# Expert tokens fetched by indirect transfers instead of one-hot products, in a mixture-of-experts decoder step

## The reference, cut to what matters

```
hid = jax.nn.silu(jnp.einsum('td,edf->tef', t, w_gate[g])) * jnp.einsum('td,edf->tef', t, w_up[g])
out = out + jnp.einsum('tef,efd->td', hid * comb[:, g, :, None], w_down[g])
```

## Time and profile before

| | us |
|---|---|
| median of 3 runs (lowest, highest) | 894.69 (891.93, 895.97) |
| the profiled execution: its time | 897.72 |
| the profiled execution: its span | 895.9 |
| rounds of layer 0, first `gate_up` to last `down` | 252.3 to 499.5 |
| rounds of layer 1 | 623.4 to about 864 |
| TensorE busy | 788.6 (88%) |
| VectorE, ScalarE, GpSimd busy | 423.2, 280.2, 128.6 |
| weight queue (q1): MB, share of the 16 DMA engines | 271.74, 77.1% |

### The profile page before, as it was taken

How to read it: one execution, slowest core, us unless ns; L and a number is a source line. 1 busy time by engine, 2 the same in 40 slices (tenths; PEclk the granted TensorE clock), 3 DMA queues, 4 the chain that set the end, 5 groups by cost and what they waited for, 6 DMA issues and landing times.

```text
span 895.9 us, 22455 instructions
## 1 busy us (share of the span) xinstructions
PE 788.6 (88%) x9194; PEld 470.6 (53%) x9195; DVE 423.2 (47%) x1134; ACT 280.2 (31%) x562; POOL 128.6 (14%) x214
## 2 busy tenths in 40 slices
PE   3799998999889999987886779976999979989984
PEld 2478886585545545443433448743545434545443
DVE  1149989515525444443331571262545434534544
ACT  2145674403223323232131251141232323223223
POOL 0160778000001010100000000000100100100001
PEclk9799997899879999999897879996999999999987
DMA  9997545428994998999999999398499999999301
GB/s 317 390 248 278 188 166 170 140 94 302 412 417 154 373 367 351 423 421 423 421 422 414 377 374 343 127 373 335 181 365 428 416 427 417 426 417 428 151 1 48
DMA packets 63885, 280.47 MB, mean 313 GB/s; under 512 B 3013, under 2 KB 3627, under 8 KB 55638
## 3 DMA queue, kind: packets, MB, share of 16 engines
q1 hardware_dynamic: 60738, 271.74, 77.1%
q0 software_dynamic: 2432, 6.94, 2.5%
q10 hardware_dynamic: 676, 1.24, 0.5%
HBM read 277.47 MB, written 3.37 MB: 313 GB/s over the span
## 4 chain that ended last, share of the span: by engine, by line
PE 66%; DMA 21%; DVE 5%; ACT 3%; SPq 2%; issue 2%; POOL 0%; POOLq 0%; DVEq 0%; ACTq 0%
PE bank L662 17%; DMA ring<-in_w_up 15%; PE bank L783 8%; PE bank L672 7%; PE bank L920 6%; PE bank L684 6%; PE bank L634 6%; DMA big<-in_w_up 3%; PE bank L529 3%; DMA ring<-in_w_ada 2%; DVE t L1260 2%; PE bank L577 2%; PE bank L569 1%; PE bank L642 1%; SPq L438 1%
## 5 line engine op out<-in xcount | busy, mean ns | idle before, releaser
L1677 DVE SCALAR_TENSOR_TENSOR x<-bank,ada,x 128x256 f32<-128x256 f32 x392 | 162.0, 476 | 0.0
L662 PE MATMUL bank<-ring,big 128*32 128x256 f32 x2112 | 136.2, 401 | 28.8 <-DMA ring<-in_w_up 22.9
L1674 DVE TENSOR_TENSOR big<-big,bank 128x32 f32<-128x32 f32 x98 | 18.4, 188 | 247.0 <-PE bank L684 247.0
L662 PEld LDWEIGHTS bank<-ring,big 128*32 128x32 f32 x2112 | 66.2, 114 | 89.4 <-issue 35.6
L1831 POOL TENSOR_TENSOR big<-t 128x192 f32<-128x192 f32 x51 | 26.5, 519 | 594.2 <-PE bank L634 430.4
L634 PE MATMUL bank<-htm,big 128*32 128x256 f32 (+1 forms) x1224 | 83.5, 386 | 4.8 <-POOL big L1834 4.8
L684 PE MATMUL bank<-big 32*128 32x264 f32 x816 | 76.6, 446 | 4.9 <-DVE x L1260 3.9
L783 PE MATMUL bank<-big,ring 128*128 128x264 f32 x320 | 73.9, 389 | 0.0
L662 PE MATMUL bank<-big 128*32 128x256 f32 x1024 | 64.3, 393 | 10.8 <-DMA big<-in_w_up 5.5
L1195 ACT ACTIVATE big<-bank 128x128 f32<-128x128 f32 x49 | 13.6, 278 | 186.3 <-PE bank L662 186.3
L529 PE MATMUL bank<-ring,cT 128*32 128x256 f32 x768 | 55.1, 435 | 16.3 <-DMA ring<-in_w_ada 11.8
(11 more groups left out here) (241 smaller groups left out, 894.1 us busy)
## 6 DMA issues: line engine op xcount, KB each, us to landing
ring<-in_w_ada SPq DMA_DIRECT2D x24, 2048.0 KB, 16.2
ring<-in_w_gate SPq DMA_DIRECT2D x21, 2048.0 KB, 23.6
ring<-in_w_up SPq DMA_DIRECT2D x21, 2048.0 KB, 25.2
ring<-in_w_down SPq DMA_DIRECT2D x21, 2048.0 KB, 27.8
big<-in_w_gate SPq DMA_DIRECT2D x11, 2048.0 KB, 18.5
big<-in_w_up SPq DMA_DIRECT2D x11, 2048.0 KB, 25.1
big<-in_w_down SPq DMA_DIRECT2D x11, 2048.0 KB, 23.4
ring<-in_w_in_even SPq DMA_DIRECT2D x5, 2048.0 KB, 33.2
```

The lines of the kernel that those rows point to most:

```text
L662: last = mm(GU[C * q:C * (q + 1), :].rearrange("p (a n) -> p a n", a=2), hgc[:, P * (k % 2) + C * (k // 2):P * (k % 2) + C * (k // 2 + 1)] ...
L1674: v.tensor_tensor(sacc[:, b], sacc[:, b], banks[:, 4:8, SEQ:T], ALU.add)
L1677: last = v.scalar_tensor_tensor(out=x[:, i, 0:SEQ], in0=bank[4 + dq][:, 0:SEQ], scalar=gate[:, i, 0:1], in1=x[:, i, 0:SEQ], op0=ALU.mult, ...
```

## The change

**Gather.** TensorE's `gather` and GpSimd's `picks` go. At the start of a layer's rounds GpSimd writes the token-major `htm` to a scratch tensor in memory, `h_rows` (four rows of 1 KB for each token). VectorE works out row numbers (`rows`, from the table `tabs`). For each chunk GpSimd issues one indirect transfer (`fetch`) of 128 rows of 1 KB into `landed`, waits for it, and copies it to `gath` (a product with ones) for TensorE's `turn`. One fetch is in flight at a time: the next is issued after that copy, and the copy waits until the chunk before has been turned.

**SwiGLU.** ScalarE uses the SiLU function; one product of VectorE goes, and `hid` is made ahead of `add_all(0)`.

**Scatter.** `gate_up` is one piece of 64 matmuls; `scatter(0)` stands behind it and `scatter(1)` behind `down`.

**Order of loads and of the start.** `ada` unit 12, the gate weights of expert 1 and unit 13 are issued ahead of units 10 and 11. In the start of layer 0's rounds, `tables()` is first and unit 14 follows it.

```
-    plan += [(("ada", 6 + i), s) for i, s in enumerate((1, 2, 3, 4, 5, 0))]
-    plan += [(("ada", 12), 1), ((0, 1, 0), 6), (("ada", 13), 2), ((0, 1, 1), 7), (("ada", 14), 3), ((0, 0, 0), 4),
+    plan += [(("ada", 6 + i), s) for i, s in enumerate((1, 2, 3, 4))]
+    plan += [(("ada", 12), 1), ((0, 1, 0), 6), (("ada", 13), 2), (("ada", 10), 5), (("ada", 11), 0), ((0, 1, 1), 7),
...
                 pe.wait_ge(E("tm_a"), 2 * TT * (l + 1))
-                gather(1)
+                tables()
                 if l == 0:
+                    ada_unit(14)
+                    ada_columns()
                     pe.wait_ge(E("ada_copied"), 5)
                 turn(1)
-                tables()
...
-                        gate_up(wgu, range(4))
+                        gate_up(wgu).then_inc(m["gu_done"], 1)
                         pe.wait_ge(m["y_copied"], g1)
                         pe.wait_ge(m["scat_ready"], g1)
                         scatter(0, g1)
-                        gate_up(wgu, range(4, KD)).then_inc(m["gu_done"], 1)
-                        gather(g2)
                         pe.wait_ge(m["hid_done"], g1)
                         tr(HT, hid, ident).then_inc(m["ht_done"], 1)
-                        scatter(1, g1)
+                        turn(g2)
                         pe.wait_ge(m["ht_copied"], g1)
-                        turn(g2)
                         pe.wait_ge(down_in[j], filled)
                         down(wd)
+                        scatter(1, g1)
...
-                    fn(sig, GU[:, 0:P], ACT.Sigmoid).then_inc(m["sig_done"], 1)
-                    act.wait_ge(m["gathered"], g2)
-                    fn(gath, GATH, ACT.Copy).then_inc(m["gath_copied"], 1)
+                    fn(silu, GU[:, 0:P], ACT.Silu).then_inc(m["silu_done"], 1)
...
+                    dve.wait_ge(m["silu_done"], g1)
+                    v.scalar_tensor_tensor(out=hid, in0=silu, scalar=tabs[:, bass.ds(NCH + g, 1)], in1=GU[:, P:2 * P],
+                                           op0=ALU.mult, op1=ALU.mult).then_inc(m["hid_done"], 1)
                     add_all(0, g1)
-                    dve.wait_ge(m["sig_done"], g1)
-                    v.tensor_tensor(sig, sig, GU[:, 0:P], ALU.mult).then_inc(m["mul_done"], 1)
...
+                def fetch():
+                    pool.indirect_dma_start(out=landed, out_offset=None, in_=h_rows,
+                                            in_offset=bass.IndirectOffsetOnAxis(ap=row_now[:, 0:1], axis=0))\
+                        .then_inc(m["fetched"], 16)
...
+                pool.dma_start(h_rows[0:4 * SEQ].rearrange("(t p q) n -> p t (q n)", t=2, q=4), htm[:, 0:2, :])\
+                    .then_inc(s_hrows, 16)
...
+                with pool.Fori(1, end) as g:
+                    g1 = pool.snap(g + 1)
+                    pool.wait_ge(m["fetched"], pool.snap(16 * g))
+                    pool.wait_ge(m["turned"], g)
+                    v.tensor_tensor(gath, landed, whole, ALU.mult).then_inc(m["gath_copied"], 1)
+                    col = rows[l][:, bass.ds(g, 1)]
+                    v.tensor_tensor(row_now[:, :], col, settled[:, 0:1], ALU.add).then_inc(m["row_set"], 1)
+                    pool.wait_ge(m["gath_copied"], g)
+                    pool.wait_ge(m["row_set"], g1)
+                    v.tensor_tensor(settled[:, 1:2], settled[:, 0:1], settled[:, 0:1], ALU.add)
+                    fetch()
```

More of the change, by code:

```diff
@@ L248, in build @@
         prow = htm[:, 2, :]
-        sig = part(P, 0)
+        silu = part(P, 0)
         hid = part(P)
@@ L256, in build @@
         hgc = part(2 * P)
-        both = part(2 * TT * C).rearrange("p (i t c) -> p i t c", i=2, t=TT)
-        pk = part(TT * C).rearrange("p (t c) -> p t c", t=TT)
+        landed = part(2 * P)
+        rowf = part(2 * (MAXCH + 1)).rearrange("p (i c) -> p i c", i=2)
         sacc = part(KD * NS).rearrange("p (r q b) -> p r q b", r=2, q=4)
@@ L285, in build @@
         tab = [sb(f"chunk_table{l}", [P, EXPERTS + 1], I32) for l in range(2)]
+        rows = [sb(f"gather_rows{l}", [P, MAXCH + 1], U32) for l in range(2)]
+        settled = sb("settled", [P, 2], U32)
+        row_now = sb("row_now", [P, 1], U32)
+        h_rows = nc.dram_tensor("h_rows", (4 * T, 2 * P), F32, kind="Internal").ap()
         onef = sb("onef", [P, EXPERTS])
@@ L464, in _ @@
             fill_expert(0, 1, 0)
-            unit_free(sp, ("ada", 13))
-            fill(("ada", 13))
+            for i in (13, 10, 11):
+                unit_free(sp, ("ada", i))
+                fill(("ada", i))
             sp.wait_ge(E("out0_done"), KD)
@@ L626, in moe @@
                 m = M[l]
[L628 to L636, removed]
                 def turn(n):
@@ L655, in tables, with gate_up @@
                     last.then_inc(m["tabs_done"], 1)
-                def gate_up(wgu, ks):
-                    for k in ks:
+                def gate_up(wgu):
+                    for k in range(KD):
                         for q in range(4):
@@ L1185, in moe @@
                 m = M[l]
[L1186 to L1188 removed]
+                act.wait_ge(m["turned"], 2)
                 copy(hgc, TURN, m["chunk_ready"])
@@ new lines, in moe @@
+                pool.wait_ge(E("tm_a"), 2 * TT * (l + 1))
+                pool.dma_start(h_rows[0:4 * SEQ].rearrange("(t p q) n -> p t (q n)", t=2, q=4), htm[:, 0:2, :])\
+                    .then_inc(s_hrows, 16)
+                pool.dma_start(h_rows[4 * SEQ:4 * T].rearrange("(p q) n -> p (q n)", q=4), htm[0:NS, 2, :])\
+                    .then_inc(s_hrows, 16)
+                pool.wait_ge(s_hrows, 32 * (l + 1))
+                pool.wait_ge(m["rows_ready"], 1)
+                v.tensor_copy(row_now[:, :], rows[l][:, 0:1]).then_inc(m["row_set"], 1)
@@ L1844, in _ @@
+                pool.wait_ge(m["fetched"], pool.snap(16 * end))
+                pool.wait_ge(m["turned"], end)
+                v.tensor_tensor(gath, landed, whole, ALU.mult).then_inc(m["gath_copied"], 1)
             moe(0)
```

57 lines of the change are left out of this document (27 added, 30 removed).

## The result

Before 894.91 us (median of 5 runs, 891.93 to 897.84), after **902.27 us** (5 runs, 901.68 to 904.12), a ratio of 1.0083 with a 95% interval of 1.0056 to 1.0110. The change makes the kernel slower by 0.8%, where I had forecast 892.2. The profiled execution after took 902.27 us with a span of 900.4; before, 897.72 and 895.9. The traces are therefore 4.5 us apart where the medians are 7.4 apart, because the profiled execution of before was 2.8 us above its own median. What follows accounts for the 4.5 us.

What follows compares the result with a forecast made beforehand. TensorE was taken to set the pace in 23 of 49 rounds, the weight queue in 26. Terms -18.4, +11.7, +0.6 and +3.6 gave -2.5 us: 895.2 profiled, 892.2 as median, range 882 to 909.

Steps and rivals of the forecast that it cites:

- 23 rounds that TensorE paces: Rounds of both layers where TensorE sets the pace, each 0.8 us shorter: -18.4 us.
- the other 26 rounds, with the fetches as traffic: Rounds where the weight queue is full: each 128 KB fetch costs 0.45 us of it, +11.7 us.
- start of the rounds: From the one-hot tables' old end to first gate_up, 10.6 us by the new path: -2.2 and +2.8, together +0.6 us.
- end of the rounds: Addition, sct and final scatter 2.3 us behind the loop, 1.8 us more for each layer: +3.6 us.
- The full queue: Begins at the last refill that found the queue empty, after ten rounds in layer 0 and four in layer 1.
- The round: Gate_up's end to down falls from 2.65 to 1.86 us, so a round falls by 0.8 us to 8.1.
- B: Rival: the fetch loop becomes the pace once a landing passes 6.0 us; +14.0 us, 909 us, chance 0.20.
- C: Rival: the fetches' traffic costs more, 0.85 us each over 26 rounds; sum +7.9, 903 us, chance 0.12.

Runs made afterwards that it cites:

- f3: The changed kernel without the two writes of h_rows and the wait for them, fetches reading a weight array instead: 899.49 us, ratio 1.0028.
- f2: The changed kernel with h_rows written in three pieces, each as soon as its part of htm is copied: 899.63 us, ratio 1.0045.
- g1: The changed kernel with each layer's first chunk gathered by one-hot products on TensorE, fetches beginning with the second chunk: 891.53 us, ratio 0.9939.
- e2: e1 with one more 16-byte transfer by GpSimd in every round, into a tile that nothing reads: 909.08 us, ratio 1.0133.
- e4: The changed kernel with fetches of 8 rows in place of 128, the other 120 rows staying zero: 887.38 us, ratio 0.9902.
- e1: The kernel before with SiLU and the new places of the scatters, the one-hot gather kept on TensorE: 906.4 us, ratio 1.0116.
- f4: The changed kernel with fetches of 512 bytes a row in place of 1 KB: 899.3 us, ratio 1.0032.

## Why the prediction was wrong, by its steps

**The sum.** By the terms of the prediction (profiled execution, us):

| term | forecast | measured |
|---|---|---|
| 23 rounds that TensorE paces | -18.4 | -23.1 |
| the other 26 rounds, with the fetches as traffic | +11.7 | +14.3 |
| start of the rounds | +0.6 | +7.5 |
| end of the rounds | +3.6 | +5.5 |
| end of the program | 0 | +3.3 |
| not assigned | 0 | -3.0 |
| sum | -2.5 | +4.5 |

The median, 902.27, lies inside the 882 to 909 that I gave, but by the width of that range alone: the forecast was a small gain and the result is a loss.

**What failed: the start of the rounds.** I wrote that "the two writes of h_rows (1.1 MB, 2.6 us of the queue) come while the weights have a lead in both layers and cost nothing". As traffic nothing speaks against it (2.8 us of queue each, and f3 gains no more than f2, with the 3 us of its layer 0 left open). But the first fetch has to wait for the write, and I had it in the path at nothing. The write's second transfer landed 10.8 us after its issue in layer 0, which the routing covered to 0.3 us, and 16.8 in layer 1, 2.75 us too long. The second part is the fetch: I took a landing of 4 us from bounds of 1.3 and 10.1, and counted from its issue it measured 5.5 in layer 1 and 6.9 in layer 0. Of the 6.9 us by which this term was missed, the landings are 4.4 and the waits for the write 2.75 and 0.3; the rest of the path was some 0.5 us shorter than I had counted. g1 takes write, fetch and copy out of the path; its trace is 10.5 us shorter than that of the changed kernel, 9.8 of them at the two starts, more than the whole loss. Of the terms that were missed this is the one with the largest share.

**What was missing: the end of the program.** No term stood for it. The trace of before could have shown only that 4.8 us lie behind the last store, not what they depend on. e2 shows it.

**The tail, mis-sized.** The chain was right: addition, `sct`, final scatter, forecast at 2.3 us behind the loop and measured at 2.26 (493.18 to 495.44 in layer 0). But I took from it the 0.5 us that the final scatter had stood behind `down`, and the loop now ends with `scatter(1)`, which itself stands behind `down`. From the last `down` to the final scatter are 2.9 and 3.0 us where there were 0.5, so 2.4 to 2.5 more and not 1.8. The rest of the 3.0 in layer 0 is the last scatter at the lower clock (1.26 us for 0.73); in layer 1 it took 1.26 before the change too.

**The full queue, begun too late in my count.** "TensorE's pace therefore counts in 10 rounds of layer 0 ahead of that point", and in 4 of layer 1: this failed. It was read from the kernel before, and the change moved the point: with rounds of 7.86 us and the fetches in the queue, the last refill that found it empty came after 4 rounds and after 2, so TensorE's pace counts in 15 rounds and a full queue in 34. What the other 8 rounds save reaches the end only as far as the queue had been idle in them, by its shares 0.14 x 55.3 + 0.15 x 18.6 = 10.5 us. The error hardly shows in the sum (-18.4 + 11.7 = -6.7 was forecast for all rounds, and -8.8 measured), because the rounds that do count saved more than forecast.

**The traffic, right in kind and in size.** 0.45 us a fetch was forecast. The queue's own records say 0.42, e4 0.49 by the length of the stretches (15.3 us back over 34 rounds, and 0.04), so the term is shown. Divided over the 26 rounds of the forecast, the +14.3 us would make 0.55; but that stage also holds what the queue had still to move at its beginning. As an estimate, 34 x 0.45 = 15.3 less those 10.5 us idle gives 4.8, near the +6.1 of the stretches in which the queue was really full.

**The round, better than forecast.** 7.86 where 8.1 stood: the stretch behind `gate_up` was 1.68 us for my 1.86, so a round saves 1.04 us in place of 0.8, and 23 x 1.04 = 23.9 against 23.1 measured in those 23 rounds, of which 14.9 in the 15 that count. The reason I gave for the saving was that gather, transpose, scatter and turn no longer fill the stretch; e1 shows that with the gather in place the rest of the edit saves nothing.

**The rivals.** B, the fetch loop as the pace, needs a loop longer than a round. In the full queue it was: GpSimd's copies at 340.90, 350.40, 359.03 and 367.89 us are 8.6 to 9.5 us apart, a round is 7.86, and the median landing over the program was 6.6. Yet TensorE waited for GpSimd's copy only at the starts of the two layers (below). While the queue was idle (262 to 281 us) fetches landed in 3.0 us and the copy waited for TensorE. From 281 to 340 us they took 7.3 (medians), above the 6.0 at which I had the cover end, while TensorE still ran rounds of 7.86. What covered this is a lead: the copy of 282.02 us is turned at 289.34, 7.3 us later, that of 340.90 at 345.35, 4.5 later. A longer stretch of this kind would have used the lead up; here the waits for weights gave it back. I had asked only for one landing against one round. C ended near the measured time (903) by luck: a fetch costs nowhere near 0.85 us, and its rows are not packets of their own, for f3's queue carries (4880 - 2432)/51 = 48 packets a fetch, not 128.
```profile
POOL big L1851 <- DMA big<-h_rows,row_now: 169.7, 29, 7.7
...
PE bank L641 <- POOL big L1851: 15.4, 2, 10.4
```
The chain of waits by pairs: total us, times, longest. The second row is all that TensorE's matmuls lost to the fetches' latency, in 49 rounds.

**What stays open.** 3.0 us fewer in the remaining stages, 1.8 of them ahead of the first routing, where the change moves only loads. Nine executions of the changed kernel and its variants with the new loads reach that point anywhere between 221.9 and 224.2 us, so I put it to the spread, without having shown it. One reading of the prediction was also loose: the slices from 358 us on move 414 to 423 GB/s only until 493 us, the last named (to 515) moves 377; nothing hangs on it.

## What to carry to other kernels

The transfers that replaced work on a busy engine were paid at three places here: where the first was waited for with nothing to cover it, as traffic where the queue was full, and at the end of the program. The first can be avoidable: do the first piece in the old way and let the transfers begin with the second; here this turned 0.8% slower into 0.6% faster. A latency is to be compared with the cover that stands in the same stretch, not with the longest latency found anywhere. And where two limits lie close, the change itself moves the point at which one gives way to the other: count the rounds again with the new round and the new traffic.

## What the runs showed of the hardware

The landing of a small transfer that GpSimd issues hardly depends on its size while weights fill the queue. Transfers from issue to landing (issues in the window, KB each, median us), first of the changed kernel from 340 to 483 us, then of e2 in the same window, then of the changed kernel from 262 to 281 us, with the queue idle, and from 281 to 340, with it full:
```profile
big<-h_rows,row_now POOLq DMA_INDIRECT x12, 6.5
```
```profile
junk<-in_c_prompt POOLq DMA_DIRECT2D x13, 0.0 KB, 5.4
```
```profile
big<-h_rows,row_now POOLq DMA_INDIRECT x3, 3.0
```
```profile
big<-h_rows,row_now POOLq DMA_INDIRECT x7, 7.3
```
From 340 to 483 us 128 KB landed in 6.5 us, 64 KB (f4) in 6.0, 8 KB (e4) in 5.8, and 16 bytes in 5.4. The 1 MB write of `h_rows` took 10 us in layer 0 and 17 in layer 1. Over the whole program the 16-byte transfer took 1.6 to 6.6 us and the fetch 2.8 to 8.6. The Trainium skill (DMA: Bandwidth & Descriptors, "Anatomy of one DMA — SWDGE (gpsimd) path") has 2.0 us plus bytes/436e3, that is 2.3 us for 128 KB as an estimate; the shortest landing, 2.8, is near it, and the medians in the full queue are 3.4 to 4.2 us above it at these four sizes. The issue of an indirect fetch holds GpSimd for 0.99 us, the plain one of e2 for 0.55. And the program's end grew by about 0.06 us for each transfer that GpSimd had issued.
